# Norm sums with the ones stationary, no diagonals and no spreading, in a two-layer hybrid decoder kernel; first down scatter a tile later; the head's first low part moved

## The chip, the cores and the metric

The kernel runs on one core of a Trainium2 chip. The metric is device microseconds of one execution; lower is better. Weights stream from HBM, everything else is held in SBUF and PSUM.

## The reference

256 tokens of 1024 channels (float32) pass two layers. Each layer has a token mixer (layer 0: gated short convolution, layer 1: causal pooling over four window sizes) and a channel mixer that looks up experts by product keys. Ahead of each of these four, and once at the end, stands an RMS norm; the first four are followed by a modulation that comes from a conditioning vector:

```python
def rmsnorm(x, g):
    y = xf * lax.rsqrt(jnp.mean(xf * xf, axis=-1, keepdims=True) + EPS)
    return (y * g.astype(jnp.float32)).astype(x.dtype)

def modulate(h, shift, scale):
    return h * (1.0 + scale[:, None, :]) + shift[:, None, :]
...
        h = modulate(rmsnorm(x, norm1_g[i]), sh1, sc1)
        ...
        x = x + g1[:, None, :] * y
        h = modulate(rmsnorm(x, norm2_g[i]), sh2, sc2)
        x = x + g2[:, None, :] * peer_ffn(h, ...)
    return rmsnorm(x, final_g)
```

The expert mixer forms queries, scores 2 x 128 keys for 8 heads, keeps the 16 best of the pair sums, and adds up 16384 experts' rows weighted by gelu(h . u) times a softmax gate; the gates of all experts that were not chosen are zero.

## The kernel before

**Layout.** Activations lie transposed: channels over the 128 partitions, in DC = 8 chunks of 256 tokens each (`X`, 128 x 2048). A sum over the channels of a token is thus a sum over partitions, which TensorE does with a column of ones.

**Weights.** Every weight tile (128 x 1024 float32) is loaded by SyncE into one of four `raw` buffers, copied by ScalarE to `high` (L461, rounded to the float32r format), and VectorE subtracts to get `low` (L725, `rest_of(n)`; `slot(n)` does it three tiles ahead). A product is three matmuls: high x moving high, high x moving low, low x moving high. The moving operand `mov` has a high part from ScalarE and a low part from VectorE. SyncE loads the tile four further on when a tile's `low` is done.

**Order of the work**, written out by hand for each engine: head (products of the conditioning vector with w_mod on VectorE, L745 and L746, summed over partitions by TensorE, L1296), norm 0, conv_in (24 tiles), conv_out (8), norm 1, query (16), up (128), down (128); then norm 2, pool_in (8), pool_group (4), pool_out (8), norm 3, query, up, down, norm 4, output. The down stage goes over the tiles in two halves of 64.

**A norm.** ScalarE squares the chunks (`square`). TensorE sums them over partitions with the square as the stationary operand and a column of ones moved (`token_sums`, L1318, two calls a chunk, one for each 128 tokens): the result lies with tokens on partitions, two columns. In norms 1 to 4 VectorE has added most squares into `total` first. ScalarE takes the square root of the two columns (L500), VectorE the reciprocal (L777), and then multiplies the identity with each column to two diagonal matrices (L780). TensorE spreads them (`spread`, L1339): ones, stationary, times a diagonal gives each token's factor on all partitions, 256 columns in the second half of `gp[:, 0]`. VectorE scales the eight chunks (L803, `scaled`), ScalarE adds the shift and rounds (L513), VectorE forms the low part (L809, `rest`), and TensorE starts the next stage's first two tiles chunk by chunk (`first_two`, L1356). Between the scaling and the reciprocal VectorE does `finish_mod` (L766, taking the modulation sums), and `gs` (L789, weight times one plus scale) in the order of its program. `keep_warm(n)` (L1313) are n small matmuls of zeros by zeros with an unused result, issued around the norms.

**The head.** Norm 0 waits on VectorE for `head_mod(1)` before its reciprocal; behind the diagonals stand `head_mod(0)` (eight products), `finish_mod`, `gs`, `rest_of(0)` (the low part of the first tile), then four scalings, `shift_last` (another `finish_mod`), and four scalings.

**Start of the down stage.** VectorE builds one-hot matrices for sets of 8 tokens (`hots`, L1055, L1057, L1061), TensorE turns two of them into gates in PSUM (`scatter`, L1518, 24 matmuls each), VectorE multiplies them into the activations (`weigh`, L1073), for the second half of the experts while the first half's down tiles run. For the other tokens the gates come from a table in HBM (`weigh_first`, L1079). `low_weight` (L1199) makes the low part of the weighted activations that the down tile moves. Two scatters stand behind the second of every eight down tiles on TensorE, and VectorE does two sets at every tile j with j % 8 == 2:

```python
for j in range(HALF):
    slot(n0 + j)
    if j + AHEAD < HALF:
        low_weight(j + AHEAD)
    if j + 2 < GROUPS:
        weigh_first(layer, j + 2)
    if j % 8 == 2:
        two_sets(1, j // 8 * 2)
```

A down tile (`down_banks`, L1569) is twelve matmuls of 512 columns.

Of the kernel before, what the change touches and what calls it, by code (L numbers as in the profile page):

```python
# [13 lines left out]
P = 128  # L14
# [78 lines left out]
def program(nc, small, x_in, k_t, w_mod, conv_in, conv_out, query, up, down, pool_in, pool_group, pool_out,  # L93
# [8 lines left out]
    with ExitStack() as ctx:  # L102
# [64 lines left out]
        sd = part(10240, TC)  # L167
        rstd = part(10240 + TC, TC)
        total = part(10240 + 3 * T, T)
        diag = part(10240 + 2 * TC, T).rearrange("p (c t) -> p c t", c=TC)  # L170
# [86 lines left out]
        diag_done, spread_done = sem("diag_done"), sem("spread_done")  # L257
# [196 lines left out]
        def _(act):  # L454
# [35 lines left out]
            def norm(k):  # L490


                if k == 0:
                    act.wait_ge(x_in_s, 16)
                    for c in range(DC):
                        square(c)
                elif k % 2:
                    act.dma_start(x_spill, flat2(X)).then_inc(spilled, 16)
                act.wait_ge(stat_done, k + 1)
                nc.scalar.activation(sd, gp[:, 0, 0:TC], ACT.Sqrt, bias=eps[:, 0:1],  # L500
                                     scale=1.0 / D).then_inc(sd_done, 1)
                if k == 4:
                    return
                if k == 0:
                    for n in range(AHEAD):
                        arrived(1, n)
                        nc.scalar.activation(flat(high[n]), tile_row(n), ACT.Copy).then_inc(high_ready, 1)
                shift = mod[:, (3 * (k % 2)) * DC:(3 * (k % 2) + 1) * DC]

                act.wait_ge(mod_taken, (2, 5, 7, 8)[k])  # L510
                for c in range(DC):
                    act.wait_ge(xr_done, DC * k + c + 1)
                    nc.scalar.activation(mov_h[:, c], xr[:, c], ACT.Identity,  # L513
                                         bias=shift[:, c:c + 1]).then_inc(mh_done, 1)
# [199 lines left out]
        def _(dve):  # L714
# [55 lines left out]
            def norm(k, shift_last=None):  # L770
# [6 lines left out]
                link(nc.vector.reciprocal(rstd, sd))  # L777

                for tc in range(TC):
                    nc.vector.tensor_scalar(diag[:, tc], eye, rstd[:, tc:tc + 1], None, ALU.mult  # L780
                                            ).then_inc(diag_done, 1)
# [11 lines left out]
                if k == 0:  # L793
                    rest_of(0)
                if k == 2:
                    rest_of(AT[1, "pool_in"] + 1)
                dve.wait_ge(spread_done, k + 1)
# [3 lines left out]
                def scaled(c):  # L801
                    dst = xr[:, c] if k < 4 else A[:, B0 + c * T:B0 + (c + 1) * T]
                    nc.vector.scalar_tensor_tensor(dst, X[:, c], weight[:, c:c + 1], gp[:, 0, T:2 * T], ALU.mult,  # L803
# [9 lines left out]
                for c in range(DC):  # L813
                    if k == 0 and c == DC // 2:
                        shift_last()
                    scaled(c)
# [281 lines left out]
            for layer in range(LAYERS):  # L1098
# [134 lines left out]
                for j in range(HALF):  # L1233
# [5 lines left out]
                    if j % 8 == 2:  # L1239
# [47 lines left out]
        def _(pe):  # L1287
# [27 lines left out]
            def token_sums(src, first, last):  # L1315

                for tc in range(TC):
                    ins = nc.tensor.matmul(gp[:, 0, tc:tc + 1], src[:, tc * P:(tc + 1) * P], ones[:, 0:1],  # L1318
                                           start=(first and tc == 0), stop=last, skip_group_check=True)
# [14 lines left out]

            def spread(k):

                for tc in range(TC):
                    pe.wait_ge(diag_done, TC * k + tc + 1)
                    ins = nc.tensor.matmul(gp[:, 0, T + tc * P:T + (tc + 1) * P], ones[:], diag[:, tc],  # L1339
                                           start=True, stop=True)  # L1340
                ins.then_inc(spread_done, 1)
# [98 lines left out]
            for layer in range(LAYERS):  # L1440
# [5 lines left out]
                spread(2 * layer)  # L1446
# [37 lines left out]
                keep_warm(12)  # L1484
                spread(2 * layer + 1)
                keep_warm(13)
# [76 lines left out]
                for half in range(2):  # L1563
# [20 lines left out]
                    if half == 0:  # L1584
                        for s in range(8):
                            down_tile(0, s, 8, s == 0)
                            if s == 1:
# [54 lines left out]
            spread(4)  # L1642
# [59 lines left out]
```

## Time and profile before

| | |
|---|---|
| median of 3 runs | 1831.64 us (1829.47 to 1831.69) |
| the profiled execution's own time | 1831.79 us |
| its span in the profile | 1830.0 us |
| TensorE, matmul, busy | 98% of the span |
| TensorE, weight load, busy | 89% |
| VectorE busy | 80% |
| ScalarE busy | 51% |
| GpSimd busy | 30% |
| mean granted TensorE clock | 0.99 of full speed |
| HBM traffic | 383 MB read, 20 MB written |

The profile is of one execution; its times are microseconds from the start of the span. PE is TensorE's matmul, PEld its weight load, DVE VectorE, ACT ScalarE, POOL GpSimd, SP SyncE. A name such as L803 is a line of the kernel. A float32 matmul call shows as two records. PEclk is the granted clock of TensorE as a share of 2.4 GHz.

### The profile page before, as it was taken

What the parts mean: (1) busy time and instruction counts of PE and PEld (TensorE: products, weight loads), DVE (VectorE), ACT (ScalarE), POOL (GpSimd) and SP (SyncE); (2) the same over time, 40 slices, a digit from 0 to 9 for tenths busy, and PEclk for the clock granted to TensorE, in tenths of its full rate; (3) what the DMA queues carried; (4) which work ended last, traced back from release to release, by engine and by line L of the source; (5) the groups of instructions that cost most, each with busy time, mean ns of one, the idle gap of its engine ahead of it and who ended that gap; (6) DMA issues with size and microseconds to landing.
All of it is one profiled execution on the core that took longest, in us unless ns stands there. A gap on an engine that the chain in (4) does not pass through costs nothing.

```text
span 1830.0 us, 35724 instructions
## 1 busy us (share of the span) xinstructions
PE 1798.5 (98%) x12373; PEld 1625.9 (89%) x12373; DVE 1465.8 (80%) x2754; ACT 927.5 (51%) x1441; POOL 547.7 (30%) x393
## 2 busy tenths in 40 slices
PE   6999999999999999999999999999999999999998
PEld 6998999999888888888889999999988888888887
DVE  7997689997787888788878768999777788875555
ACT  3344455555555444444555546555555544445543
POOL 1000037778862111000000002777787521110000
PEclk9999999999999999999999999999999999999999
DMA  8898779767665766788845745766766677665552
GB/s 318 323 346 304 263 253 248 194 173 185 183 162 176 241 229 224 276 334 315 316 153 194 260 157 163 194 172 184 186 176 169 173 248 224 225 232 189 191 194 92
DMA packets 148974, 404.34 MB, mean 221 GB/s; under 512 B 50592, under 2 KB 50976, under 8 KB 148256
## 3 DMA queue, kind: packets, MB, share of 16 engines
q1 hardware_dynamic: 105456, 384.21, 59.7%
q0 software_dynamic: 43008, 16.93, 8.5%
q10 hardware_dynamic: 432, 2.23, 0.3%
q8 instruction: 40, 0.66, 0.1%
q14 instruction: 38, 0.31, 0.1%
HBM read 383.25 MB, written 20.05 MB: 220 GB/s over the span
## 4 chain that ended last, share of the span: by engine, by line
PE 94%; DVE 4%; DMA 1%; ACT 1%; issue 0%; SPq 0%; DVEq 0%; ACTq 0%
PE acc L1569 37%; PE ps L1382 31%; PE ps L1399 8%; PE acc L1399 5%; PE ps L1402 4%; PE gp L1518 3%; PE acc L1402 2%; PE ps L1356 1%; DVE acts L746 1%; DVE low L725 1%; PE gp L1507 1%; PE gp L1296 1%; DMA acts<-w_mod 1%; DVE acts L1151 0%; DVE acts L803 0%
## 5 line engine op out<-in xcount | busy, mean ns | idle before, releaser
L725 DVE TENSOR_TENSOR low<-raw,high 128x1024 fp32r<-128x1024 f32 x596 | 726.7, 1221 | 265.0 <-ACT high L461 256.9
L461 ACT ACTIVATE high<-raw 128x1024 fp32r<-128x1024 f32 x593 | 626.5, 1057 | 414.6 <-PE acc L1569 336.2
L426 POOL DMA_INDIRECT table<-added x256 | 473.7, 1851 | 768.1 <-DVE added L944 628.1
L1569 PE MATMUL acc<-high,mov 128*128 128x512 f32 x2048 | 637.2, 390 | 1.6 <-DVE mov L1199 1.4
L1382 PE MATMUL ps<-mov,high 128*128 128x256 f32 x3296 | 600.0, 285 | 1.8 <-DVE acts L1110 1.4
L1382 PEld LDWEIGHTS ps<-mov,high 128*128 128x128 f32 x3296 | 517.3, 193 | 2.3 <-DVE low L725 1.5
L1382 PE MATMUL ps<-mov,low 128*128 128x256 f32 x1648 | 468.2, 284 | 0.0
L1569 PEld LDWEIGHTS acc<-high,mov 128*128 128x128 f32 x2048 | 384.5, 188 | 83.3 <-issue 2.6
L1569 PE MATMUL acc<-low,mov 128*128 128x512 f32 x1024 | 398.4, 389 | 0.0
L1382 PEld LDWEIGHTS ps<-mov,low 128*128 128x128 f32 x1648 | 318.1, 193 | 0.0
L1569 PEld LDWEIGHTS acc<-low,mov 128*128 128x128 f32 x1024 | 192.3, 188 | 38.8
L595 ACT ACTIVATE acts<-ps 128x256 f32<-128x256 f32 x160 | 61.2, 382 | 196.8 <-PE ps L1382 192.1
L1399 PE MATMUL ps<-mov,high 128*128 128x512 f32 x592 | 149.1, 394 | 0.0
L438 POOL DMA_DIRECT2D mov<-table x96 | 51.7, 539 | 250.5 <-DVE acts L1079 226.1
L1399 PEld LDWEIGHTS ps<-mov,high 128*128 128x128 f32 x592 | 106.3, 189 | 19.3
L746 DVE SCALAR_TENSOR_TENSOR acts<-acts,cact 128x1024 f32<-128x1024 f32 x86 | 110.0, 1279 | 4.5 <-DMA acts<-w_mod 4.0
L1199 DVE TENSOR_TENSOR mov<-acts,mov 128x256 fp32r<-128x256 f32 x256 | 106.5, 418 | 2.3 <-ACT mov L648 2.3
L648 ACT ACTIVATE mov<-acts 128x256 fp32r (+1 forms) x256 | 101.8, 400 | 12.0 <-DVE acts L1079 12.0
L1399 PE MATMUL acc<-mov,high 128*128 128x512 f32 x384 | 97.0, 394 | 0.0
L1402 PEld LDWEIGHTS ps<-mov,low 128*128 128x128 f32 x592 | 80.7, 190 | 5.9
L476 ACT ACTIVATE acts<-ps 128x256 f32 (+1 forms) x76 | 29.3, 386 | 106.1 <-PE ps L1402 101.5
L1402 PE MATMUL ps<-mov,low 128*128 128x256 f32 x592 | 82.5, 282 | 0.0
(139 smaller groups left out, 1387.5 us busy)
## 6 DMA issues: line engine op xcount, KB each, us to landing
raw<-up SPq DMA_DIRECT2D x256, 512.0 KB
raw<-down SPq DMA_DIRECT2D x256, 512.0 KB
acts<-w_mod SPq DMA_DIRECT2D x84, 512.0 KB, 5.1
raw<-query SPq DMA_DIRECT2D x32, 512.0 KB
table<-hot SPq DMA_DIRECT2D x32, 512.0 KB, 6.5
raw<-conv_in SPq DMA_DIRECT2D x24, 512.0 KB
mov<-table POOLq DMA_DIRECT2D x96, 128.0 KB, 3.8
acts<-w_mod SPq DMA_DIRECT2D x6, 1024.0 KB, 15.4
```

The costliest lines, as they stand in the source:

```text
L426: nc.gpsimd.indirect_dma_start(table[layer], bass.IndirectOffsetOnAxis(ap=DEST[:, col:col + 1], axis=0), GT0[:, col:col + 1], None, comput ...
L461: nc.scalar.activation(flat(high[s]), tile_row(s), ACT.Copy).then_inc(high_ready, 1)
L595: nc.scalar.activation(A[:, bass.ds(i * (RING * T) + (first + s) * T, T)], ps[:, s % 2, 0:T], ACT.Gelu).then_inc(evac_act, 1)
L648: nc.scalar.activation(mov_h[:, s], A[:, bass.ds(g * T, T)] if not isinstance(g, int) else A[:, g * T:(g + 1) * T], ACT.Copy).then_inc(wh_ ...
L725: nc.vector.tensor_tensor(flat(low[n % RING]), tile_row(n % RING), flat(high[n % RING]).bitcast(F32), ALU.subtract).then_inc(low_ready, 1)
L746: return nc.vector.scalar_tensor_tensor(macc[:, m], tile, c, macc[:, m], ALU.mult, ALU.add)
L1199: nc.vector.tensor_tensor(mov_l[:, s], A[:, g * T:(g + 1) * T], mov_h[:, s].bitcast(F32), ALU.subtract).then_inc(wl_ready, 1)
L1382: ins = nc.tensor.matmul(dst, w[s][:, c], m[:, mv], start=(first and n == 0), stop=(last and n == 2), skip_group_check=skip)
L1399: nc.tensor.matmul(b, high[s][:, c], flat(mov[:, c]), start=(c == 0), stop=(c == DC - 1), skip_group_check=True)
L1402: ins = nc.tensor.matmul(b[:, 0:T], low[s][:, c], mov_h[:, c], start=False, stop=(c == DC - 1), skip_group_check=True)
L1518: ins = nc.tensor.matmul(gp[:, u, j * HALF:(j + 1) * HALF], hot2[:, u, j // 2, :, j % 2], hot1[:, u, j // 2, n, :, j % 2], start=(n == 0), ...
L1569: ins = nc.tensor.matmul(acc[:, b, :], w[:, s, tok], flat(v[s])[:, cols], start=(opening and n == 0), stop=(closing and n == 2), skip_grou ...
```

## The change

The norm's sums take the ones as the stationary operand and move the squares, so that the sum of every token comes out on all partitions, in the 256 columns that the spread filled before. The square root and the reciprocal then work on 128 x 256, in place in `sd`, and the scaling reads `sd` from SBUF rather than the spread from PSUM. The diagonals, the spread and their semaphores are gone. The fillers of 12 and 13 around the spread of norms 1 and 3 become one of 17. In norm 0 `rest_of(0)` and `shift_last` stand behind the second scaling. At the start of each layer's down stage the first two scatters stand behind the third tile, and VectorE's first two sets behind the work of j = 3.

```diff
@@ -164,10 +164,9 @@
         xr = part(13312, DC * T).rearrange("p (c t) -> p c t", c=DC)
         SQ0 = 11264
         sq = part(SQ0, DC * T).rearrange("p (c t) -> p c t", c=DC)
-        sd = part(10240, TC)
-        rstd = part(10240 + TC, TC)
         total = part(10240 + 3 * T, T)
-        diag = part(10240 + 2 * TC, T).rearrange("p (c t) -> p c t", c=TC)
+
+        sd = part(10240, T)
         vp = part(B0, 2 * (T + 2)).rearrange("p (s t) -> p s t", s=2)
         cs = part(B0 + 1024, 2 * T).rearrange("p (s t) -> p s t", s=2)
         cv = part(B0 + 1536, 3 * T).rearrange("p (s t) -> p s t", s=3)
@@ -254,7 +253,6 @@
         acc_out_dve = sem("acc_out_dve")
         back = sem("back")
         step = sem("step")
-        diag_done, spread_done = sem("diag_done"), sem("spread_done")
         total_done, half_done = sem("total_done"), sem("half_done")
         stored = sem("stored")
 
@@ -497,7 +495,7 @@
                 elif k % 2:
                     act.dma_start(x_spill, flat2(X)).then_inc(spilled, 16)
                 act.wait_ge(stat_done, k + 1)
-                nc.scalar.activation(sd, gp[:, 0, 0:TC], ACT.Sqrt, bias=eps[:, 0:1],
+                nc.scalar.activation(sd, gp[:, 0, T:2 * T], ACT.Sqrt, bias=eps[:, 0:1],
                                      scale=1.0 / D).then_inc(sd_done, 1)
                 if k == 4:
                     return
@@ -774,11 +772,7 @@
                 if k == 0:
                     head_mod(1)
                 dve.wait_ge(sd_done, k + 1)
-                link(nc.vector.reciprocal(rstd, sd))
-
-                for tc in range(TC):
-                    nc.vector.tensor_scalar(diag[:, tc], eye, rstd[:, tc:tc + 1], None, ALU.mult
-                                            ).then_inc(diag_done, 1)
+                link(nc.vector.reciprocal(sd, sd))
                 if k == 0:
                     head_mod(0)
                     finish_mod(0, (1,))
@@ -790,17 +784,14 @@
                     weight = gs[:]
                 else:
                     weight = sm[:, C_FG:C_FG + DC]
-                if k == 0:
-                    rest_of(0)
                 if k == 2:
                     rest_of(AT[1, "pool_in"] + 1)
-                dve.wait_ge(spread_done, k + 1)
                 if k < 4:
                     shift = mod[:, (3 * (k % 2)) * DC:(3 * (k % 2) + 1) * DC]
 
                 def scaled(c):
                     dst = xr[:, c] if k < 4 else A[:, B0 + c * T:B0 + (c + 1) * T]
-                    nc.vector.scalar_tensor_tensor(dst, X[:, c], weight[:, c:c + 1], gp[:, 0, T:2 * T], ALU.mult,
+                    nc.vector.scalar_tensor_tensor(dst, X[:, c], weight[:, c:c + 1], sd, ALU.mult,
                                                    ALU.mult).then_inc(xr_done, 1)
 
                 def rest(c):
@@ -811,7 +802,8 @@
                                                    ALU.subtract).then_inc(ml_done, 1)
 
                 for c in range(DC):
-                    if k == 0 and c == DC // 2:
+                    if k == 0 and c == 2:
+                        rest_of(0)
                         shift_last()
                     scaled(c)
                 if k == 0:
@@ -1236,7 +1228,7 @@
                         low_weight(j + AHEAD)
                     if j + 2 < GROUPS:
                         weigh_first(layer, j + 2)
-                    if j % 8 == 2:
+                    if j % 8 == (2 if j >= 8 else 3):
                         two_sets(1, j // 8 * 2)
                 for g in range(AHEAD):
                     low_weight(HALF + g)
@@ -1314,9 +1306,9 @@
 
             def token_sums(src, first, last):
 
-                for tc in range(TC):
-                    ins = nc.tensor.matmul(gp[:, 0, tc:tc + 1], src[:, tc * P:(tc + 1) * P], ones[:, 0:1],
-                                           start=(first and tc == 0), stop=last, skip_group_check=True)
+
+                ins = nc.tensor.matmul(gp[:, 0, T:2 * T], ones[:], src, start=first, stop=last,
+                                       skip_group_check=True)
                 if last:
                     ins.then_inc(stat_done, 1)
 
@@ -1331,14 +1323,6 @@
                 pe.wait_ge(total_done, (k // 2 + 1) * (DC - 2))
                 token_sums(total, True, False)
                 square_sums(k, DC - 1, DC)
-
-            def spread(k):
-
-                for tc in range(TC):
-                    pe.wait_ge(diag_done, TC * k + tc + 1)
-                    ins = nc.tensor.matmul(gp[:, 0, T + tc * P:T + (tc + 1) * P], ones[:], diag[:, tc],
-                                           start=True, stop=True)
-                ins.then_inc(spread_done, 1)
 
             moved = [0]
 
@@ -1443,7 +1427,6 @@
                     square_sums(0, 0, DC)
                     pe.wait_ge(macc_done, 1)
                     sum_mod((1,))
-                spread(2 * layer)
                 if layer == 1:
                     keep_warm(13)
                 if layer == 0:
@@ -1481,9 +1464,7 @@
                     sum_mod((4,))
                     run(1, "pool_out", 8, evac_dve, 44)
                     total_sums(3)
-                keep_warm(12)
-                spread(2 * layer + 1)
-                keep_warm(13)
+                keep_warm(17)
                 run(layer, "query", 16, evac_act, out_act, True)
                 n0 = AT[layer, "up"]
 
@@ -1584,7 +1565,7 @@
                     if half == 0:
                         for s in range(8):
                             down_tile(0, s, 8, s == 0)
-                            if s == 1:
+                            if s == 2:
                                 scatter(1, 0, 0, 2)
                                 scatter(1, 0, 1, 2)
                         with pe.Fori(0, HALF // 8 - 1) as i:
@@ -1639,7 +1620,6 @@
                 square_sums(2 * layer + 2, DC // 2, DC)
                 next_scale(5, DC)
                 keep_warm(12 if layer else 4)
-            spread(4)
 
 
 # ---- launch: one core ----
```

## Rows read from the trace of the kernel before

**Rows 1.** The page of the profile, part 4: the chain that ended last, by engine.

```profile
PE 94%; DVE 4%; DMA 1%; ACT 1%; issue 0%; SPq 0%; DVEq 0%; ACTq 0%
```

**Rows 2.** Groups by line and shape (busy us, mean ns | idle); one timeline row of scores.

```profile
L476 ACT ACTIVATE acts<-ps 128x256 f32 x64 | 24.7, 386 | 89.8 <-PE ps L1402 85.2 <-issue 4.6
L926 DVE RECIPROCAL acts<-acts 128x2 f32<-128x2 f32 x16 | 2.3, 146 | 0.0
L734 DVE RECIPROCAL ctmp<-ctmp 128x8 f32<-128x8 f32 x1 | 0.2, 203 | 0.0
L735 DVE TENSOR_TENSOR cact<-ctmp,sm 128x8 f32<-128x8 f32 x1 | 0.2, 167 | 0.0
...
199.86 1.06 PE L1507 MATMUL gp<-acts 128*128 128x128 f32 x8
```

**Rows 3.** Timeline of the final norm: start us, us, engine, line, tiles, [idle before].

```profile
1819.60 2.30 PE L1318 MATMUL gp<-ones,acts 128*128 128x1 f32 x16 [0.59 <-ACT acts L488]
1821.93 0.26 ACT L500 ACTIVATE acts<-gp,eps 128x2 f32<-128x2 f32 x1 [1.21 <-PE gp L1318]
1822.29 0.17 DVE L777 RECIPROCAL acts<-acts 128x2 f32<-128x2 f32 x1 [2.03 <-ACT acts L500]
1824.19 3.22 DVE L803 SCALAR_TENSOR_TENSOR acts<-acts,sm,gp 128x256 f32<-128x256 f32 x8 [1.22 <-PE gp L1339]
```

**Rows 4.** Timeline of the second query norm.

```profile
1017.69 0.26 ACT L500 ACTIVATE acts<-gp,eps 128x2 f32<-128x2 f32 x1 [0.69 <-PE gp L1318]
1019.55 3.22 DVE L803 SCALAR_TENSOR_TENSOR acts<-acts,gs,gp 128x256 f32<-128x256 f32 x8 [0.81 <-PE gp L1339]
1020.78 0.55 PE L1356 MATMUL ps<-mov,high 128*128 128x256 f32 x1
```

**Rows 5.** Timeline of the first query norm.

```profile
141.11 0.26 ACT L500 ACTIVATE acts<-gp,eps 128x2 f32<-128x2 f32 x1 [1.75 <-PE gp L1318]
143.34 3.22 DVE L803 SCALAR_TENSOR_TENSOR acts<-acts,gs,gp 128x256 f32<-128x256 f32 x8 [1.11 <-PE gp L1339]
144.57 0.55 PE L1356 MATMUL ps<-mov,high 128*128 128x256 f32 x1
```

**Rows 6.** Timeline of the pool norm, VectorE's part.

```profile
951.09 1.23 DVE L725 TENSOR_TENSOR low<-raw,high 128x1024 fp32r<-128x1024 f32 x1
952.23 3.21 DVE L803 SCALAR_TENSOR_TENSOR acts<-acts,gs,gp 128x256 f32<-128x256 f32 x8
```

**Rows 7.** The head: timeline, and busy times from 22.05 to 44.70 by windows.

```profile
21.45 0.17 DVE L777 RECIPROCAL acts<-acts 128x2 f32<-128x2 f32 x1
22.05 0.74 DVE L745 TENSOR_SCALAR acts<-acts,cact 128x1024 f32<-128x1024 f32 x1
44.86 0.47 PE L1382 MATMUL ps<-mov,high 128*128 128x256 f32 x2 [1.37 <-DVE acts L1110]
...
22.05:44.70 22.65, 20.35 (x182) 19.80 (x182) 22.06 (x35) 9.19 (x14) 0.00 (x0) 0.92 0.76 290
```

**Rows 8.** Timeline of the down start, both layers; one row of the chain for tiles.

```profile
585.29 0.90 PE L1518 MATMUL gp<-hot 128*128 128x64 bf16 x24 [1.11 <-DVE hot L1061]
587.10 0.90 PE L1518 MATMUL gp<-hot 128*128 128x64 bf16 x24 [0.91 <-DVE hot L1061]
...
588.09 0.42 DVE L1199 TENSOR_TENSOR mov<-acts,mov 128x256 fp32r<-128x256 f32 x1
600.13 0.41 DVE L1199 TENSOR_TENSOR mov<-acts,mov 128x256 fp32r<-128x256 f32 x1
...
768.02 163.50 PE acc L1569 x720
...
1460.86 0.90 PE L1518 MATMUL gp<-hot 128*128 128x64 bf16 x24 [0.79 <-DVE hot L1061]
```

**Rows 9.** Windows around the two query norms: busy times, then PEclk, DMA share, GB/s.

```profile
142.00:148.30 6.30, 6.29 (x34) 6.04 (x35) 5.18 (x15) 4.37 (x9) 0.00 (x0) 0.50 0.33 138
1019.00:1022.10 3.10, 3.10 (x22) 2.85 (x21) 2.55 (x7) 1.97 (x5) 0.00 (x0) 0.50 0.91 383
```


## The prediction

> **What bounds the kernel.** I read the chain of waits first: 94% of the span hangs on TensorE and 4% on VectorE [rows 1]. So only stretches in which TensorE waits, or runs at half clock, can be shortened, and anything put into them is paid in full. The change touches seven: five norms (head, before the query tiles of both layers, before pool_in, final) and the start of the down stage of both layers. I then read each as a timeline. In every norm no tile can start until the sums have gone through ScalarE (sqrt), VectorE (reciprocal), and back through TensorE (spread); this loop is pure latency.
>
> **The one new price that matters: a wide reciprocal.** Before, the reciprocal works on two columns; after, the square root and the reciprocal work on all 256. The other VectorE work on 256 columns costs about 0.4 us whatever it does, but for the reciprocal the rows speak against that [rows 2]. Two columns take 146 ns [rows 2], or 170 where the next instruction waits for it [rows 3]; eight columns take 203 ns, while an ordinary operation on eight columns takes 167. So columns are dear: (203 - 170)/6 = 5.5 ns or (203 - 146)/6 = 9.5 ns each. For 256 columns, 203 ns + 248 x 5.5 = 1.57 us to 203 ns + 248 x 9.5 = 2.56 us. Below that stands only the ordinary price, some 0.4 us, by the 256-column row of ScalarE (386 ns). I take 2.2 us, from the upper half of the two slopes, since the sixteen rows behind the 146 weigh more than the rounded 170, and rows of the same operation are nearer than a row of another.
>
> The Trainium skill, page "VectorE: DVE Perf Modes", section "Walkthrough: the 8-slice pipeline in each mode", says that the reciprocal is an iterated divide with a repeat count of 8; this speaks against the change. Read as eight clocks an element at the 0.96 GHz that its page "Trainium Kernel Development and Optimization" gives (NeuronCore Architecture), it would be 8.3 ns a column (an estimate), and the sum below 0.3 us longer; no run here shows a wide one.
>
> The square root grows from 0.26 us [rows 3] to the 0.39 us of a 256-column read of PSUM [rows 2]: +0.13.
>
> **The sums.** Each chunk was two calls, four records of 128 weight columns and one moved column; it becomes one call with 256 moved columns. Float32 calls show two records each: 4 calls that move 128 columns are 8 records in 1.06 us [rows 2], one about every 0.11 us. 256 columns then are 2 x 0.22 = 0.44 us, against 16 records in 2.30 us for four chunks, 0.57 each [rows 3]. So four chunks shrink by some 0.35 us in the final norm, of which the last has to follow its square, by 0.2 where the squares arrive one by one, by 0.1 where two chunks are left.
>
> **Norm by norm**, from the start of the square root to the first scaling (L803). The new loop is 0.39 + 0.10 (hand-over, 1821.93 + 0.26 to 1822.29 [rows 3]) + 2.2 + 0.03, and where gs (L789) is computed 0.2 more: gs stood beside the spread, now it stands behind the reciprocal in VectorE's order.
> - Final: 1821.93 to 1824.19 is 2.26 us [rows 3]; new 2.72. +0.46, less 0.35 of the sums: **+0.1**.
> - Second query norm: 1017.69 to 1019.55 is 1.86 us [rows 4]; new 2.92. +1.05 less 0.1: **+0.95**.
> - First query norm: 141.11 to 143.34 is 2.23 us [rows 5], as the spread fell into the low clock; new 2.92. +0.7 less 0.1: **+0.6**.
> - Pool norm: the spread was hidden here. Behind the diagonals VectorE does two mod additions, gs and a tile's low part (951.09, 1.23 us), and the scaling starts right behind at 952.23 without a wait in its row [rows 6]. So removing the spread gains nothing; removing the diagonals gains 0.4 (0.60 less the 0.17 and 0.03 of the reciprocal, next item). +2.03 for the reciprocal, +0.13, -0.4, -0.2: **+1.55**.
> - Head: VectorE is busy 22.06 of the 22.65 us from 22.05 to 44.70, and TensorE then waits 1.4 us for its copy L1110 [rows 7]. What VectorE gets before 22.05 shifts all of it. Reciprocal and diagonals took from 21.45 to the first w_mod product at 22.05 = 0.60 us [rows 7]; new 2.23: **+1.6**. The sums and the square root lie under the arrival of w_mod and cost nothing.
>
> **The head's low part** (one of 1.2 us, L725) is only moved on VectorE, from before the first scaling to behind the second, with shift_last two scalings earlier. It lets ScalarE and TensorE begin about half a microsecond sooner, but VectorE's row of work up to 44.70 is the same length, and TensorE waits there: **0**. It has no DMA in it and passes no queue but VectorE's. If that cover went (VectorE no longer last), it would give back up to 0.5.
>
> **Down start.** In layer 0 the two scatters behind tile 1 are held by the hot matrices: idle 1.11 us before 585.29 and 0.91 before 587.10 [rows 8]. With tile 2 in between (2.73 us, 163.50 over 60 tiles [rows 8]), both matrices are ready and some 2 us of waiting go. What is late next: tile 3 needs its low weight, 588.09 + 0.42 = 588.5, about when the scatters end (tile 1's end at 585.29 - 1.11 = 584.2, + 2.73 + 1.5 = 588.4). Then tiles 3 to 6 run to 588.5 + 4 x 2.73 = 599.4. Tile 7 needs its low parts, and the two sets of weighing and hot matrices, which now stand behind tile 6's work rather than before it, still stand before tile 7's: its low weight ends at 600.13 + 0.41 = 600.5 as before [rows 8]. TensorE waits 1.1 us and is then 0.95 ahead of the old 601.5 (587.10 + 0.73 + 5 x 2.73): **-0.95**. Layer 1 has one wait of 0.79 us between its scatters [rows 8], and about 0.1 of issue around it; tiles 3 to 7 just meet their low parts: **-0.9**. Bounds of the two: 0 (all given back before tile 7) to -3. The rest of the stage is TensorE's alone, so the gain stays. No load is issued later; tile 6's buffer even frees sooner, by the two sets' work.
>
> **Clock.** The spread, and the filler around it, go; one filler of 17 is issued behind the sums. TensorE then idles some 3 us until the first moving chunk. The granted clock is 0.50 from 142.0 to 148.3 and from 1019.0 to 1022.1 [rows 9], that is 1.2 GHz, and every matmul takes twice as long there as at 2.4. The first query norm has 3.8 us of tile work at 1.2 GHz (144.57 to 148.3 [rows 5, 9]), the second 1.4 (1020.78 to 1022.1 [rows 4, 9]); what came before the rise was filler and tiles, no idling. If the second becomes like the first: (3.8 - 1.4) x 0.5 = +1.2. I take **+0.8** for both norms together, bounds -0.8 (a later start meets a risen clock) and +2.5. In the pool norm and the head VectorE covers it.
>
> **Sum.** 0.1 + 0.95 + 0.6 + 1.55 + 1.6 = +4.8; -1.85 down start; +0.8 clock: **+3.75 us**. The profiled execution took 1831.79 us (span 1830.0 and 1.8 around it), 0.15 over the median of 1831.64. 1831.8 + 3.75 = **1835.5**.
>
> **Rivals.**
> 1. *The reciprocal is as cheap as other operations* (0.42 us). Then the loop with one hop less pays: 5 x 1.78 = 8.9 less, and with idling of 1.2 us instead of 3 no clock term: 3.75 - 8.9 - 0.8 = -5.95, **1825.8**. For it: every other VectorE row costs about 1 ns a column. Against it: the eight-column row, one sample, though. It decides from a wide reciprocal of about 0.9 us downward (3.75 - 0.8 - 5 x 1.3 = -3.55, the 0.2% below). Chance 0.16.
> 2. *The clock decides*: with TensorE idle behind the sums, the query tiles start cold in both layers and, in the head, the shift sums (sixteen records of one column, at 2.30 us for sixteen [rows 3]) run at half clock, some 1.5 us longer, behind the idling that the later head brings; VectorE then stalls for mod behind the low part. 3.75 + 1.7 + 1.5 = +6.95, **1838.7**. For it: both query norms already see the low clock [rows 9]. Against: the fillers of 80 and 20 stay. Chance 0.14.
> 3. *The down scatter's gain is given back* at tile 7 in both layers (two sets late, no gain): +1.85, **1837.4**. For it: in layer 0 half of it is; against: layer 1's VectorE has gaps. Chance 0.10.
> 4. *The reciprocal is at the low slope*, 1.57 us, and the clock costs nothing: 3.75 - 5 x 0.63 - 0.8 = -0.2, **1831.6**. This is where the forecast turns into "no change". Chance 0.18.
> The forecast itself has the remaining 0.42.
>
> **Numbers.** Forecast 1835.5; its own range with the slopes' ends and the clock's is 1833 to 1838.5. The range that holds 8 in 10 takes in rival 4 and most of 2, 1830.8 to 1839, and leaves out rival 1. A measurement of this kernel can tell about 0.2% (3.7 us) from no change, and the forecast lies just on that line, a little over half of its own cases beyond it: with rivals 2 and 3 slower 0.47; same 0.36 (rival 4, the lower half of the forecast); faster 0.17.
>
> **What would show it.** Right: one reciprocal of 256 columns per norm of 2.2 us (1.6 to 2.6) on VectorE; a square root of 0.39; no L1339 records; the sums as two records of about 0.22 us a chunk; the first scaling of the second query norm 2.9 us behind the square root's start; TensorE idle about 3 us behind the filler; project L1382 of the head starting near 46.5; scatters of the first down tiles without a wait, then about 1 us of waiting at tile 7 of layer 0. Wrong: a reciprocal of under 1 us makes it rival 1, and the time falls under 1828; 1.2 GHz reaching past both first query tiles makes it rival 2; a copy L1110 no later than before would mean that the head was not VectorE's.

## The result and the profile after

The changed kernel took 1833.58 us (median of 22 runs, 1831.70 to 1837.09) against 1829.88 us before (22 runs on the same chips, 1827.00 to 1833.79): ratio 1.0019, 95% interval 1.0013 to 1.0025, that is +3.5 us (+2.4 to +4.6). The forecast was +3.75 us, in a range of 1830.8 to 1839.0, and put 0.47 on slower and 0.36 on a difference within 0.2%. The measured difference of 0.19% lies on that line, a shade inside. As a time the forecast was 1835.5, 1.9 us too long, because it was counted from one execution of 1831.8 us, and the median of the kernel before is 1829.88. In the two profiled executions the spans are 1830.0 and 1832.4 us.

Groups by line and shape of the changed kernel (busy us, mean ns of one, idle before); L775 is the reciprocal, L498 the square root, L1310 the sums, L732 the eight-column reciprocal of the head:

```profile
L1310 PE MATMUL gp<-acts,ones 128*128 128x256 f32 x44 | 13.9, 460 | 11.6 <-ACT acts L486 11.2 <-ACT acts L538 0.4
L775 DVE RECIPROCAL acts<-acts 128x256 f32<-128x256 f32 x5 | 8.8, 1753 | 7.0 <-ACT acts L498 6.8
L498 ACT ACTIVATE acts<-gp,eps 128x256 f32<-128x256 f32 x5 | 2.4, 473 | 9.0 <-PE gp L1310 9.0
L732 DVE RECIPROCAL ctmp<-ctmp 128x8 f32<-128x8 f32 x1 | 0.2, 204 | 0.0
```

The wide reciprocal takes 1.75 us; (1753 - 204)/248 = 6.2 ns a column, where [rows 2] allowed 5.5 to 9.5. It is the dear operation of the change. The square root takes 0.47 us, not 0.39. A chunk's sum in the final norm takes 1.99/4 = 0.50 us, where 0.44 was forecast.

The chain that ended last, of the page of the changed kernel, against [rows 1]:

```profile
PE 91%; DVE 5%; DMA 2%; issue 1%; ACT 1%; SPq 0%; DVEq 0%; ACTq 0%
```

Timeline of the second query norm after (start us, us, engine, line, tiles, idle before), to be read against [rows 4]:

```profile
1019.74 0.47 ACT L498 ACTIVATE acts<-gp,eps 128x256 f32<-128x256 f32 x1 [0.79 <-PE gp L1310]
1020.25 1.75 DVE L775 RECIPROCAL acts<-acts 128x256 f32<-128x256 f32 x1 [1.75 <-ACT acts L498]
1022.03 0.17 DVE L783 SCALAR_TENSOR_TENSOR gs<-mod,sm 128x8 f32<-128x8 f32 x1
1022.24 3.25 DVE L794 SCALAR_TENSOR_TENSOR acts<-acts,gs 128x256 f32<-128x256 f32 x8
1023.47 0.36 PE L1340 MATMUL ps<-mov,high 128*128 128x256 f32 x1 [2.82 <-ACT mov L511]
```

From the square root's start to the scaling it is 2.50 us (before 1.86). TensorE has nothing to do for 2.82 us ahead of the first tile. The pool norm after, VectorE and TensorE, against [rows 6]:

```profile
950.12 1.75 DVE L775 RECIPROCAL acts<-acts 128x256 f32<-128x256 f32 x1 [0.80 <-ACT acts L498]
952.38 1.22 DVE L723 TENSOR_TENSOR low<-raw,high 128x1024 fp32r<-128x1024 f32 x1
953.52 3.25 DVE L794 SCALAR_TENSOR_TENSOR acts<-acts,gs 128x256 f32<-128x256 f32 x8
954.74 0.55 PE L1340 MATMUL ps<-mov,high 128*128 128x256 f32 x1 [3.71 <-ACT mov L511]
```

The final norm, against [rows 3], and the head's third tile, against [rows 7]:

```profile
1822.28 1.99 PE L1310 MATMUL gp<-acts,ones 128*128 128x256 f32 x8 [0.59 <-ACT acts L486]
1824.31 0.47 ACT L498 ACTIVATE acts<-gp,eps 128x256 f32<-128x256 f32 x1 [0.91 <-PE gp L1310]
1824.88 1.75 DVE L775 RECIPROCAL acts<-acts 128x256 f32<-128x256 f32 x1 [1.93 <-ACT acts L498]
1826.67 3.26 DVE L794 SCALAR_TENSOR_TENSOR acts<-acts,sm 128x256 f32<-128x256 f32 x8
...
20.68 1.75 DVE L775 RECIPROCAL acts<-acts 128x256 f32<-128x256 f32 x1
45.59 0.47 PE L1366 MATMUL ps<-mov,high 128*128 128x256 f32 x2 [2.22 <-DVE acts L1102]
```

Down start of layer 0 after, against [rows 8]: both scatters are one row, with no wait in front.

```profile
588.70 1.63 PE L1499 MATMUL gp<-hot 128*128 128x64 bf16 x48
```

**Where the time went.** The same points of the work in both profiled executions:

| point | before | after | difference | this step |
|---|---|---|---|---|
| third tile of conv_in starts | 44.86 | 45.59 | +0.73 | +0.73 |
| third query tile, layer 0 | 152.24 | 154.27 | +2.03 | +1.30 |
| first down tile, layer 0 | 578.46 | 580.43 | +1.97 | -0.06 |
| eleventh down tile, layer 0 | 611.35 | 611.01 | -0.34 | -2.31 |
| third pool_in tile | 960.76 | 962.72 | +1.96 | +2.30 |
| third query tile, layer 1 | 1027.41 | 1030.91 | +3.50 | +1.54 |
| first down tile, layer 1 | 1453.63 | 1457.08 | +3.45 | -0.05 |
| eleventh down tile, layer 1 | 1485.09 | 1487.65 | +2.56 | -0.89 |
| final scaling starts | 1824.19 | 1826.67 | +2.48 | -0.08 |

So the norms lose 5.9 us and the down stages win 3.2, in this pair. Four norms are dearer, the final one costs nothing. Steps of two single traces are good to about 1 us at best, as the sections below show: a table's landing and TensorE's clock change them from one execution to the next.

### The profile page after: what moved, and what is told of

Same layout as the page of the kernel before. It is cut to its first block, busy times and chain, and to the rows that moved or that the text cites. A ratio compares the mean times of both kernels' runs of the same rounds, so it can differ in the third digit from the quotient of the medians.

```text
span 1832.4 us, 35553 instructions
## 1 busy us (share of the span) xinstructions
PE 1790.6 (98%) x12293; PEld 1616.5 (88%) x12293; DVE 1470.4 (80%) x2744; ACT 928.0 (51%) x1441; POOL 547.1 (30%) x393
## 4 chain that ended last, share of the span: by engine, by line
PE 91%; DVE 5%; DMA 2%; issue 1%; ACT 1%; SPq 0%; DVEq 0%; ACTq 0%
PE acc L1550 38%; PE ps L1366 28%; PE ps L1383 7%; PE acc L1383 5%; PE ps L1386 4%; PE gp L1499 3%; PE acc L1386 2%; DVE acts L744 2%; DMA acts<-w_mod 2%; PE ps L1340 1%; DVE low L723 1%; PE gp L1288 1%; PE gp L1488 1%; DMA raw<-conv_in 1%; DVE acts L775 0%
## 5 line engine op out<-in xcount | busy, mean ns | idle before, releaser
L723 DVE TENSOR_TENSOR low<-raw,high 128x1024 fp32r<-128x1024 f32 x596 | 726.0, 1220 | 264.0 <-ACT high L459 262.1
```

The costliest lines, as they stand in the source:

```text
L723: nc.vector.tensor_tensor(flat(low[n % RING]), tile_row(n % RING), flat(high[n % RING]).bitcast(F32), ALU.subtract).then_inc(low_ready, 1)
```

## The experiments

The theory after the result was this: the norms lose because 256 columns of reciprocal (1.75 us) take the place of two columns, two diagonals and a spread; the down edit wins about 0.9 a layer. The rival was that the loss is TensorE's clock, which falls because TensorE has nothing to do meanwhile, so that what fills the wait matters as much as its length. All ratios are against the kernel before, on the same chips, with 95% intervals; 0.001 is 1.8 us. Differences in us are taken from the ratios where they are against the kernel before, and from the medians where they are against the changed kernel.

### Each half alone

The kernel before with the down edit only:

```diff
-                    if j % 8 == 2:
+                    if j % 8 == (2 if j >= 8 else 3):
...
-                            if s == 1:
+                            if s == 2:
                                 scatter(1, 0, 0, 2)
```

> The kernel before with only the down stage changed: the first two scatters behind tile 2 and VectorE's first two sets behind the work of j = 3, norms and head as before. If the forecast's term holds, 1.9 us less than before (0.95 in layer 0, 0.9 in layer 1). By the trace after it would be 3.2 us less (2.3 and 0.9). Rival, that the later scatter is given back at tile 7: no change. In its profile: no wait before L1518 in the first ten tiles, and a wait of about 1 us at tile 7 of layer 0 by the forecast, none by the trace after.

1827.08 us, ratio 0.9984 (0.9975 to 0.9993): 2.9 us less (1.3 to 4.6). It pays, but the time cannot tell 1.9 from 3.2; the trace can. Timeline of TensorE at the down start of layer 0 in this kernel:

```profile
584.30 1.63 PE L1518 MATMUL gp<-hot 128*128 128x64 bf16 x48
586.13 0.47 PE L1569 MATMUL acc<-high,mov 128*128 128x512 f32 x1 [0.21 <-DVE mov L1199]
...
598.17 0.47 PE L1569 MATMUL acc<-high,mov 128*128 128x512 f32 x1 [0.87 <-DVE mov L1199]
```

The scatters no longer wait, and tile 7 waits for its low weight, about 1 us, as the forecast had it. From the start of the first down tile to that of the eleventh it is 32.89 us before and 31.88 here: 1.0 won. The 2.31 of the changed kernel's trace hold something else: in layer 0 of the kernel before, and in this one, VectorE waited 1.3 and 1.2 us at its weighing L1079 for a piece of the gate table to land; in the changed kernel's trace it did not. That wait comes and goes between executions:

```profile
582.01 0.43 DVE L1079 TENSOR_TENSOR acts<-acts,mov 128x256 f32<-128x256 f32 x1 [1.31 <-DMA mov<-table]
```

(kernel before, timeline of VectorE, layer 0). Where it is absent, the stretch is 31.46 us with the old order (kernel before, layer 1; 31.46 to 31.51 in three more such stretches of the runs below) and 30.54 to 30.59 with the new one, in all 17 such stretches of the traces with the down edit: 0.9 won a layer, and TensorE waits at no tile. So the size of the forecast's term holds, but its wait of 1 us at tile 7 shows only here, in layer 0, where the table landed late.

The changed kernel with the down edit taken back (the same edit reversed):

> The changed kernel with its down stage put back as before: norms and head changed only. If the down stage saves 1.9 to 3.2 us, this is 5.5 to 7 us slower than before; the rival, that the down stage saves nothing, has it at the changed kernel's own +3.7. In its profile the two waits before L1518-like scatters of the first down tiles are back.

1835.95 us, ratio 1.0031 (1.0020 to 1.0043): 5.7 us slower than before (3.7 to 7.9), 2.4 more than the changed kernel. With the run above it adds up within the intervals: +5.7 for norms and head and -2.9 for down make +2.8, and +3.5 (2.4 to 4.6) was measured together. Of the two old waits in layer 0 one is back in this trace, 0.79 us before the second scatter; the table did not land late there.

### The reciprocal

The changed kernel with this line left out, so that the scaling multiplies by the root mean square and not by one over it:

```diff
                 dve.wait_ge(sd_done, k + 1)
-                link(nc.vector.reciprocal(sd, sd))
```

> The changed kernel without the wide reciprocal: the scaling multiplies by the square root itself, so the five reciprocals of 1.75 us are left out and all else stays. If the reciprocals are on the path in all five norms: 5 x 1.78 = 8.9 us less than the changed kernel, so about 5.2 less than before (1824.7), and some more where TensorE's idling gets shorter and the clock stays up. Rival, that the clock and the idling set the norms' cost whatever VectorE does: at most 4 to 5 us less than the changed kernel, about as before. Where VectorE's work in the head was covered, the third tile of conv_in starts as before, else 1.8 us earlier.

1822.15 us, ratio 0.9957 (0.9944 to 0.9969): 7.9 us less than before, 11.4 less than the changed kernel, more than the 8.9 expected of five reciprocals. The rival's bound of 4 to 5 fell. In the head the third tile of conv_in starts 1.5 us earlier (44.05), so VectorE's work was hardly covered there. The other 2.5 us are about what TensorE's clock gives back: with the waits shorter, the first two tiles behind the three norms took 6.62, 7.33 and 6.19 us instead of 7.59, 7.98 and 7.44 (measured as in the section on the filler below), 2.9 us in all. The sums of the first query norm took 1.11 us instead of 2.05, but other executions of the changed norm show 1.11 as well (see the clock, below), so that part is chance. Against both, the stretch from that third tile to the first query norm's modulation sums is 1.0 us longer in this trace.

Can the reciprocal go and the result stay? ScalarE has a table function for one over the square root, and can take it in the pass that it makes anyway:

```diff
-                nc.scalar.activation(sd, gp[:, 0, T:2 * T], ACT.Sqrt, bias=eps[:, 0:1],
+                nc.scalar.activation(sd, gp[:, 0, T:2 * T], ACT.Abs_reciprocal_sqrt, bias=eps[:, 0:1],
...
                 dve.wait_ge(sd_done, k + 1)
-                link(nc.vector.reciprocal(sd, sd))
```

(and the same function in the two table loads).

> The changed kernel with ScalarE taking one over the square root in its one step (another function of its tables), and no reciprocal on VectorE; the same computation. If only the reciprocal's 1.75 us made the wide norms a loss, this has the time of the run without the reciprocal, about 7.9 us less than before (1822), and is the fastest version. Rival, that the other function's table costs loads or more time a column on ScalarE: 0.5 to 3 us above that.

1823.94 us, ratio 0.9968 (0.9956 to 0.9980): 5.9 us less than before and 9.6 less than the changed kernel. Whether the 1.8 us to the run without any reciprocal are real is open, since the intervals overlap; neither the activation (0.473 us) nor the table loads (1.28 us each, as many as in the changed kernel) are dearer. Groups of this kernel:

```profile
L498 ACT ACTIVATE acts<-gp,eps 128x256 f32<-128x256 f32 x5 | 2.4, 473 | 8.7 <-PE gp L1309 8.7
```

The final norm in this kernel (timeline) shows the loop as the change meant it, 0.58 us from the function's start to the scaling, where it was 2.26 before and is 2.36 in the changed kernel:

```profile
1814.17 0.47 ACT L498 ACTIVATE acts<-gp,eps 128x256 f32<-128x256 f32 x1 [0.91 <-PE gp L1309]
1814.75 3.26 DVE L793 SCALAR_TENSOR_TENSOR acts<-acts,sm 128x256 f32<-128x256 f32 x8 [1.94 <-ACT acts L498]
```

So the sums with the ones stationary are a good idea; the wide reciprocal behind them is not.

### The filler and the clock

The changed kernel with more filler while TensorE waits:

```diff
-                    keep_warm(13)
+                    keep_warm(55)
...
-                keep_warm(17)
+                keep_warm(50 if layer else 33)
```

> The changed kernel with more filler while TensorE waits for ScalarE and VectorE: 33 matmuls of zeros behind the sums of the first query norm and 50 behind the second (17 in both before), 55 in the pool norm (13 before). If the idling of 2 to 4 us is why the first two tiles run at 1.2 GHz, the stretch of those tiles falls from 7.5 to 8.0 us to about 6.2 us in each of the three norms, and the time by 2 to 4 us, to about 1830. Rival, that the low clock comes of the norm's own single and float32 matmuls: no change, or up to 1 us slower where the filler ends after the first moving chunk is ready.

1830.76 us, ratio 1.0004 (0.9995 to 1.0013): 2.8 us less than the changed kernel. And from the other side, the kernel before without the filler around the spread in the query norms and behind it in the pool norm:

```diff
-                if layer == 1:
-                    keep_warm(13)
...
-                keep_warm(12)
                 spread(2 * layer + 1)
-                keep_warm(13)
```

> The kernel before without the filler around the spread in the two query norms and behind it in the pool norm; everything else as before. If idling of TensorE sets the clock of the first two tiles, their stretch grows from the 6.2 to 7.7 us of before to the 7.4 to 8.0 of the changed kernel, and the time by 1 to 2.5 us. Rival, that the filler does nothing for the clock: no change.

1833.73 us, ratio 1.0020 (1.0011 to 1.0029): 3.7 us slower (2.0 to 5.3), more than the 1 to 2.5 expected. Idling of TensorE alone, without one instruction added, costs this kernel as much as the whole change did. What it costs is seen in the stretch of the first two tiles behind each norm (first matmul of L1356 or L1340 to the next tile), by the timelines:

| stretch, us | before | down only | changed | filler | before, no filler | one table step |
|---|---|---|---|---|---|---|
| query, layer 0 | 7.67 | 6.17 | 7.59 | 6.20 | 7.45 | 6.20 |
| pool_in | 7.31 | 7.31 | 7.98 | 7.33 | 7.44 | 7.34 |
| query, layer 1 | 6.63 | 6.17 | 7.44 | 6.20 | 7.57 | 6.20 |

The matmuls are the same, so the difference is the clock. Windows over the second query stretch (length, busy PE, PEld, DVE, ACT, POOL, granted clock, DMA share, GB/s), one row each of the changed kernel, of the one with filler and of the kernel before without:

```profile
1023.47:1030.91 7.44, 7.44 (x48) 7.30 (x49) 6.41 (x15) 5.72 (x12) 0.00 (x0) 0.77 0.01 2
```

```profile
1021.36:1027.56 6.20, 6.20 (x49) 5.92 (x49) 6.10 (x15) 5.74 (x12) 0.00 (x0) 1.00 0.05 21
```

```profile
1023.82:1031.39 7.57, 7.57 (x48) 7.43 (x49) 6.39 (x15) 5.72 (x12) 0.00 (x0) 0.76 0.02 6
```

The granted clock is 0.77 in the changed kernel, 1.00 with the filler and 0.76 in the kernel before without it; the number of matmuls is the same to one record. The low clock need not stand right behind the wait. In the changed kernel TensorE idled for 2.82 us, ran six records at full clock, and then fell to 1.2 GHz while it was busy:

```profile
1023.47:1024.20 0.73, 0.73 (x6) 0.73 (x7) 0.73 (x3) 0.73 (x3) 0.00 (x0) 1.00 0.00 0
1024.28:1027.50 3.22, 3.22 (x18) 3.22 (x17) 3.22 (x10) 3.19 (x7) 0.00 (x0) 0.50 0.02 5
```

Chance has a large part in it. In the kernel before, the first query stretch took 7.67 us in one execution and, with the same norm code, 6.17 in the run with the down edit only. The sums of the first query norm, which stand ahead of the filler, differ in the same way. The same four records took 2.05 us in the changed kernel and 1.11 in the run with the head's low part put back, whose norm code is the same (windows, columns as above):

```profile
140.79:142.84 2.05, 2.05 (x7) 1.50 (x8) 0.17 (x1) 0.00 (x0) 0.00 (x0) 0.50 1.06 432
```

```profile
141.25:142.36 1.11, 1.11 (x9) 0.92 (x9) 0.17 (x1) 0.00 (x0) 0.00 (x0) 1.00 0.98 395
```

The times on record show how much of the result is the clock. Each execution has its mean granted clock. In the 68 executions of the kernel before that were taken with the experiments it is 0.9912 on average, in the 22 of the changed kernel 0.9892, and a clock lower by 0.001 goes with a time longer by 1.0 us in the one and 1.2 in the other. So of the difference of some 3.5 us about 2.0 go with the clock, and 1.8 (1.2 to 2.3) are left between executions of equal clock (an estimate, from a common slope). At a granted clock of 0.990 the medians are 1832.2 (14 executions) and 1832.9 (6), at 0.989 they are 1832.0 (6) and 1833.6 (8). The spread from run to run (1827 to 1834) follows the clock too: the kernel before has a median of 1828.9 at 0.993.

### Orders on VectorE

The changed kernel with the head's low part and `shift_last` back in their old places:

```diff
+                if k == 0:
+                    rest_of(0)
...
-                    if k == 0 and c == 2:
-                        rest_of(0)
+                    if k == 0 and c == DC // 2:
                         shift_last()
```

> The changed kernel with the head's first low part and shift_last back where they were (low part ahead of the first scaling, shift_last behind the fourth). The forecast puts this edit at nothing, since VectorE's row of work ends at the same time: time as the changed kernel within 0.3 us, the third tile's first matmul at the same distance from the reciprocal's start (24.9 us). Rival, that the earlier start of ScalarE and TensorE is worth something: 0.5 us slower than the changed kernel. The rounds cannot tell 0.5 us; the distance in the profile can.

1833.53 us, ratio 1.0019 (1.0011 to 1.0028), the changed kernel's. From the reciprocal's start to the third tile it is 24.80 us against 24.91 with the edit, and with the edit it is 24.65 in three other traces and 24.98 in a fourth: worth nothing within 0.2 us, as forecast.

What does not need the square root put ahead of it:

```diff
+                if k % 2:
+                    make_gs()
+                if k == 2:
+                    rest_of(AT[1, "pool_in"] + 1)
                 dve.wait_ge(sd_done, k + 1)
                 link(nc.vector.reciprocal(sd, sd))
...
-                if k == 2:
-                    rest_of(AT[1, "pool_in"] + 1)
```

> The changed kernel with VectorE's work that does not need the square root put ahead of the reciprocal: gs in the two query norms, the tile's low part in the pool norm. If that work stands on the path behind the wide reciprocal, as the timeline says: 0.2 + 0.2 us less in the query norms and 0.8 less in the pool norm (the low part of 1.2 us, of which 0.8 fit into VectorE's wait), 1.2 in all, to about 1832.4. Rival, that TensorE's clock hides it: the distance from the square root's start to the scaling shrinks but the time does not.

1831.98 us, ratio 1.0016 (1.0007 to 1.0025); not told apart from the changed kernel (1.0019). The distances from square root to scaling shrink as expected (2.56 to 2.36, 3.98 to 3.08, 2.50 to 2.36 us), but in the profiled execution the clock took it back: the second query stretch is 8.68 us, the longest seen, at a granted clock of 0.64. An edit of a few tenths in front of an unfilled wait was thus not decidable by time here.

### Together

Filler and that order, arithmetic as in the changed kernel (30, 47 and 43 matmuls):

> The changed kernel with both edits that leave its arithmetic alone: filler through the wait (30, 47, 43 matmuls) and gs and the low part ahead of the reciprocal. If the two are independent, 2.8 + 1.2 to 1.6 us less than the changed kernel: 1829.3, 0.7 less than before, the reciprocals' cost then just paid by the down stage. Rival, that the run with gs ahead gained by chance: 1830.8 as with the filler alone.

1830.61 us, ratio 1.0000 (0.9991 to 1.0009), the same as with filler alone within the noise. That is the rival's number (1830.8), not the expected 1829.3, though all three stretches are at their shortest (6.20, 7.33, 6.20 us). The 1.2 us of the order edit are not resolved.

And with the one table step:

> The run with one table step (no reciprocal) with gs and the pool norm's low part ahead of the wait, and filler sized to the shorter wait (28 in the query norms, 25 in the pool norm): all edits that paid together. 0.2 + 0.2 + 0.8 us less than that run, and the first two tiles at their shortest (6.2, 7.3 and 6.2 us): 1822.7, some 7.2 us less than before. Rival, that the shorter wait leaves VectorE's row in the pool norm as long as it was: 0.4 only, 1823.5.

1821.64 us, ratio 0.9948 (0.9934 to 0.9961): 9.5 us less than before (expected 7.2) and the fastest of all, in five executions. It is better than the table step alone by 2.3 us in the medians and 3.7 in the ratios, where 1.2 was expected; the intervals overlap a little. It does not win everywhere yet: in its first query norm the 28 filler matmuls ran at the low clock and outlasted the wait:

```profile
142.96 3.19 PE L1310 MATMUL acc<-zeros 128*128 128x128 bf16 x28
143.20 0.47 ACT L498 ACTIVATE acts<-gp,eps 128x256 f32<-128x256 f32 x1 [3.43 <-PE gp L1315]
143.78 3.25 DVE L799 SCALAR_TENSOR_TENSOR acts<-acts,gs 128x256 f32<-128x256 f32 x8 [2.13 <-ACT acts L498]
```

The first tile started 2.13 us behind the scaling's start instead of 1.23, 0.9 us lost. The sums ahead of that filler ran at the low clock too, 2.05 us.

## Why the prediction was right, and where its terms were not

The total was right (+3.75 against +3.5), and so was the mechanism that it named first: a wide reciprocal that costs more than the diagonals and the spread it replaces. That the total came so close is partly luck. Without the clock the forecast's terms make +2.95, and about +2.0 was measured; its clock term was +0.8, and the traces show about +2.3. The reciprocal taken too dear and the clock taken too cheap cancelled.

- **Price of the reciprocal.** Taken as 2.2 us, measured 1.75: too dear by 0.45 in five norms, about 2.2 us. The error is the weight given to the sixteen two-column rows behind which nothing waits; the one with a wait behind it (0.17) and the eight-column row give 5.5 ns a column, and 6.2 was measured. By the repeat count of eight that the Trainium skill gives (page "VectorE: DVE Perf Modes", section "Walkthrough: the 8-slice pipeline in each mode"), read as eight clocks an element as in the prediction, it would have been some 8.3 ns, an estimate; the measurement decides against that reading.
- **Square root.** 0.47 instead of 0.39, 0.08 too cheap in each of the four norms behind the head. The copy of 256 columns (386 ns) was the wrong row to take it from, and not because of the function: the square root reads its bias from SBUF, one value a partition, and a copy from PSUM with such an operand (a scale from `sm`) stood in the trace of the kernel before at 472 ns:

```profile
L567 ACT ACTIVATE mov<-ps,sm 128x256 fp32r<-128x256 f32 x8 | 3.4, 472 | 2.5 <-PE ps L1382 2.4
```

- **The loop in each norm.** Forecast +0.46, +1.05, +0.7 (final, second, first query), measured from square root to scaling +0.10, +0.64, +0.33, all by the same 0.4: the reciprocal's error less the square root's. The pool norm gained 1.40 in this distance (2.58 to 3.98), forecast 1.75; two other traces of the old pool norm have 2.90 and 2.89, from which it would be 1.1. The step "gs stood beside the spread, now it stands behind the reciprocal" held.
- **Sums.** Forecast -0.35 in the final norm; measured from the first sum to the square root 2.33 to 2.03, -0.30. Held there. In the first query norm it is 1.07 us from the first sum to the square root before and 2.09 after, +1.0 us that no term had. That is the clock of this pair and not the form of the sums: the eight one-column records before took 1.03 us at a granted clock of 1.00, the four wide ones after 2.05 at 0.50. At 1.00 the wide ones take 1.11 (the run with the head's low part put back), and at 0.50 the one-column records take 1.85 (the kernel before without filler). So both forms feel the low clock, and at equal clock they differ by 0.1 us at 1.00 and 0.2 at 0.50.
- **Head.** Forecast +1.6, measured +1.50 from the reciprocal's start to the third tile (23.41 to 24.91), though the reciprocal started 0.77 us earlier in that execution. The reciprocal brought 1.19 of it (22.47 - 20.68 against 0.60). The other 0.3 belong to the execution: VectorE was busy for 24.02 of 24.82 us, with a wait of 0.17 that was not there before, and in three other traces with the same head the distance is 24.65, +1.24.
- **Clock.** Forecast +0.8 for the two query norms, and "in the pool norm VectorE covers it". For the query stretches that held in this pair (-0.08 and +0.81), with a large share of chance. What failed is the pool norm, put at nothing: its stretch grew by 0.67 us at a granted clock of 0.71 instead of 0.96, behind a wait of TensorE of 3.71 us. The sums of the first query norm, also put at nothing, lost 0.9 to the clock in this execution. The run with filler puts what the clock takes in the changed kernel at 2.8 us, and the rival "the clock decides" had named this cause with +3.2 on top of the forecast. A smaller error is the step "every matmul takes twice as long": in the first query norm the records of the first tiles start 0.21 us apart at 0.50 and 0.12 at 1.00 (timeline of the kernel before), a factor of 1.8.
- **Down start.** Forecast -0.95 and -0.9, measured -1.0 (with the table's landing late) and -0.9 wherever it is not. The size held. The way to it in layer 0 was read from an execution with a late landing: the waits of 1.11 and 0.91 us of [rows 8] belong to it, and so does the wait of 1 us at tile 7 that was to give half of the gain back. Without a late landing there is one wait of 0.79 before and none after, in layer 0 as in layer 1. The -2.31 of the one pair is that landing, late by chance in the kernel before.
- **Head's low part.** Forecast 0, measured 0 (24.80 and 24.91 us).

With the measured sizes: loops 0.10 + 0.64 + 0.33 + 1.40 = +2.5, sums at full clock +0.1 - 0.3 = -0.2, head +1.5, down -1.8, together +2.0; and the clock, by the three stretches over the shortest seen (6.17, 7.31, 6.17), 3.4 us in the changed kernel against 2.0 in the kernel before, +1.4, and +0.9 in the first query norm's sums. That is +4.3, inside the measured +2.4 to +4.6, and its two parts are near the 1.8 and 2.0 that the granted clocks of all executions give. The clock term changes with the execution, so the sum cannot be closed better than that.

## What to carry to other kernels

A hop between engines that is saved is worth its latency only if the work moved into its place is not wider: price the operation at its new width, and from rows of the same operation at two widths, not from others of that width. A wait of TensorE has two prices, its length and the clock behind it; fill it, but with filler that ends before the wait does even at the low clock. Compare down to the single wait before calling a difference of two traces the edit's: here 1.3 us were the landing of a table. And set the granted clocks of all executions beside their times before giving a difference to the program's own waits: here about half of it went with the clock.

## What was unexpected

- A reciprocal on VectorE costs 6.2 ns a column (1.753 us for 256, 0.204 for 8); the scaling of the same rows takes 3.25/(8 x 256) = 1.6 ns a column and the split L723 1.2.
- ScalarE's square root of 256 columns from PSUM takes 0.473 us against 0.386 for a copy of the same shape. One over the square root takes the same 0.473, and a copy with one scale value a partition 0.472: the operand costs the 0.09 us, not the function.
- Removing the 25 filler matmuls at each query norm and the 13 of the pool norm, which compute nothing, made the kernel before 3.7 us slower.
